# Expert weights in another buffer order, with two 4 MB loads for the second half of the second pair's gate/up rows

## The reference

```python
h = rmsnorm(x, norm2_g) * (1 + sc2) + sh2
logits = h @ w_router + b_router              # 32 experts, top 4 per token, softmax over those
for e in range(32):
    gu = h @ w_gu[e] + b_gu[e]                # w_gu[e]: 1024 x 2048 float32, 8 MB
    g, u = split(gu)                          # clamped
    hdn = (u + 1) * (g * sigmoid(1.702 * g))
    y = hdn @ w_down[e] + b_down[e]           # w_down[e]: 1024 x 1024 float32, 4 MB
    acc = acc + comb[:, e] * y
x = x + g2 * acc
```

## Time and profile before

| | us |
|---|---|
| median of 3 runs | 1290.95 |
| lowest and highest run | 1288.82, 1293.2 |
| the profiled execution | 1290.43 |
| its span, first to last instruction | 1288.7 |
| PE busy | 1212.8 (94%) |
| DVE busy | 407.5 (32%) |
| ACT busy | 200.6 (16%) |
| POOL busy | 33.1 (3%) |
| moved by DMA | 475.21 MB, mean 369 GB/s |

### The profile page before, as it was taken

How to read it: one execution, slowest core, us unless ns; L and a number is a source line. 1 busy time by engine, 2 the same in 40 slices (tenths; PEclk the granted TensorE clock), 3 DMA queues, 4 the chain that set the end, 5 groups by cost and what they waited for, 6 DMA issues and landing times.

```text
span 1288.7 us, 14118 instructions
## 1 busy us (share of the span) xinstructions
PE 1212.8 (94%) x5542; PEld 581.2 (45%) x5542; DVE 407.5 (32%) x781; ACT 200.6 (16%) x402; POOL 33.1 (3%) x50
## 2 busy tenths in 40 slices
PE   5999999999999999999999998989999998989997
PEld 1777478888644343333333333433333333334332
DVE  5178895895312211130121112121301211121213
ACT  3222004230221010011101001100111010011000
POOL 3300100001000000000000000000000000000000
PEclk9999999999999999999999999999999999999999
DMA  9943442779599899999999999999999999999995
GB/s 376 379 176 132 137 169 95 311 289 385 229 379 426 347 428 430 425 429 426 426 430 428 428 426 429 426 429 426 429 426 426 429 429 428 426 428 425 429 425 232
DMA packets 53539, 475.21 MB, mean 369 GB/s; under 512 B 3986, under 2 KB 4146, under 8 KB 23939
## 3 DMA queue, kind: packets, MB, share of 16 engines
q1 hardware_dynamic: 52370, 471.26, 88.1%
q0 software_dynamic: 1136, 3.51, 0.9%
HBM read 473.70 MB, written 1.05 MB: 368 GB/s over the span
## 4 chain that ended last, share of the span: by engine, by line
PE 67%; DMA 28%; DVE 2%; ACT 1%; issue 1%; SPq 0%; DVEq 0%
PE bank L1170 20%; PE bank L1269 12%; DMA area_sb<-w_down 11%; DMA ring_sb<-w_down 11%; PE bank L874 10%; PE bank L1125 4%; PE bank L1285 4%; PE bank L1028 3%; PE bank L883 3%; DMA area_3h_sb<-w_down 3%; DMA ring_sb<-w_gu 2%; PE bank L1069 2%; PE bank L1139 1%; DVE area_sb L1896 1%; PE bank L799 1%
## 5 line engine op out<-in xcount | busy, mean ns | idle before, releaser
L1170 PE MATMUL bank<-ring_sb,area_sb 128*64 128x512 f32 x1152 | 341.5, 599 | 5.6 <-DMA area_3h_sb<-w_gu 5.4
L1170 PE MATMUL bank<-area_sb 128*64 128x512 f32 x768 | 232.5, 599 | 11.4 <-DMA ring_sb<-w_gu 11.4
L1269 PE MATMUL bank<-ring_sb,area_sb 128*64 128x512 f32 x512 | 175.9, 603 | 22.6 <-DMA area_sb<-w_down 7.2
L1170 PEld LDWEIGHTS bank<-ring_sb,area_sb 128*64 128x64 f32 x1152 | 103.6, 137 | 137.9 <-issue 136.1
L874 PE MATMUL bank<-area_3h_sb,ring_sb 128*128 128x256 f32 x704 | 154.2, 379 | 0.0
L874 PEld LDWEIGHTS bank<-area_3h_sb,ring_sb 128*128 128x128 f32 x704 | 133.2, 190 | 20.1 <-issue 1.8
L1170 PEld LDWEIGHTS bank<-area_sb 128*64 128x64 f32 x768 | 70.3, 138 | 158.8 <-issue 158.8
L1269 PE MATMUL bank<-area_sb 128*64 128x512 f32 x352 | 109.1, 600 | 10.5 <-DMA area_sb<-w_down 10.5
L2155 DVE TENSOR_SCALAR area_sb<-bank 128x512 f32<-128x512 f32 x32 | 22.1, 691 | 278.1 <-PE bank L1170 278.1
L1269 PEld LDWEIGHTS bank<-ring_sb,area_sb 128*64 128x64 f32 x512 | 51.8, 138 | 121.7 <-issue 104.3
L2179 DVE TENSOR_TENSOR area_sb<-area_sb,bank 128x512 f32<-128x512 f32 x64 | 44.0, 687 | 172.8 <-PE bank L1285 172.8
(11 more groups left out here) (281 smaller groups left out, 882.7 us busy)
## 6 DMA issues: line engine op xcount, KB each, us to landing
ring_sb<-w_gu SPq DMA_DIRECT2D x72, 2048.0 KB, 30.4
area_sb<-w_gu SPq DMA_DIRECT2D x48, 2048.0 KB, 26.3
ring_sb<-w_down SPq DMA_DIRECT2D x32, 2048.0 KB, 30.4
area_sb<-w_down SPq DMA_DIRECT2D x22, 2048.0 KB, 20.7
ring_sb<-w_in SPq DMA_DIRECT2D x14, 2048.0 KB, 10.5
ring_sb<-w_ada SPq DMA_DIRECT2D x12, 2048.0 KB, 10.6
area_3h_sb<-w_down SPq DMA_DIRECT2D x8, 2048.0 KB, 39.0
area_3h_sb<-w_gu SPq DMA_DIRECT2D x8, 2048.0 KB, 39.1
```

The costliest lines, as they stand in the source:

```text
L1170: ins = pe.matmul(bank[n][r, :], xT[:, k, r], w[e][:, n * 512:(n + 1) * 512], start=False, stop=k == KT - 1, skip_group_check=True)
L1269: ins = pe.matmul(bank[4 + n][r, :], hidT[:, k, e * SLOTS:(e + 1) * SLOTS], w[e][:, kk // 2, kk % 2, n * 512:(n + 1) * 512], start=False, ...
```

## The change

1. `SLOT_OF` is a new order of the buffers, so that chunks 16 and 18 (the second half of the gate/up rows of pair b's first expert) lie in buffers 0 and 1 and chunks 17 and 19 (those of its second expert) in 2 and 3, side by side.
2. In all bodies but the last, each of these two pairs of chunks is one load of 4 MB (`load_four_rows`), issued in the place of chunk 16 and of chunk 17, once both buffers are free; chunks 18 and 19 have no load of their own. PE waits for all four before k 4 of pair b and no more at k 6.
3. Channels are interleaved by four: partition p holds rows 4p to 4p + 3 of 512. The 4 MB load thus has 32 KB in one stretch for each partition; the other gate/up loads take two of the four rows, 16 KB out of each 32 KB. The turns, the gathers, the modulation columns, the router's rows and its gain follow with a step of 4.
4. Eight chunks instead of ten are loaded ahead in the loop (`AHEAD`). Before the first body ten loads are still issued, in the order `FIRST_AHEAD`: chunks 0 to 7, 12 and 13, which go to buffers 0 to 9. The first body is written out, without the loads that have been made.
5. The last turn of h2 waits for the last piece of x before its first transpose, where two of its four could start a piece earlier.

```diff
@@ -49,7 +49,10 @@
 PAIR_CHUNKS = 12
 BODY_CHUNKS = 2 * PAIR_CHUNKS
-SLOT_OF = list(range(MOE_SLOTS)) + list(range(7)) + [7, 8, 9] + [3, 4, 5, 6]
+SLOT_OF = [0, 1, 2, 3, 4, 5, 6, 7] + [0, 1, 2, 3, 8, 9, 4, 5] + [0, 2, 1, 3, 6, 7, 8, 9]
+AHEAD = 8
+FIRST_AHEAD = [0, 1, 2, 3, 4, 5, 6, 7, 12, 13]
 FAR = 4096.0
 F32 = mybir.dt.float32
@@ -518,10 +521,13 @@
         def moe_chunk_landed(b, c):
             return moe_landed[SLOT_OF[PAIR_CHUNKS * b + c]]
-        def wait_moe_chunk(eng, i, b, c):
+        def wait_moe_chunk(eng, i, b, c, p):
             n = PAIR_CHUNKS * b + c
-            eng.wait_ge(moe_chunk_landed(b, c), i * (16 * SLOT_OF.count(SLOT_OF[n]))
-                        + 16 * SLOT_OF[:n + 1].count(SLOT_OF[n]))
+            slot = SLOT_OF[n]
+            fewer = slot in (SLOT_OF[PAIR_CHUNKS + 6], SLOT_OF[PAIR_CHUNKS + 7])
+            eng.wait_ge(moe_landed[slot], i * (16 * (SLOT_OF.count(slot) - fewer)) + fewer * 16 * p
+                        + 16 * SLOT_OF[:n + 1].count(slot))
         def moe_bank(name):
             return bank[6 + MISC_NO[name] % 2]
@@ -610,69 +616,96 @@
                 e0 = j * 4 + 2 * b
                 e = c % 2
+                flat = moe_flat[SLOT_OF[PAIR_CHUNKS * b + c]]
                 if c < 8:
-                    row = 2 * P * (c // 2)
-                    src = a["w_gu"][0, bass.ds(e0 + e, 1), row:row + 2 * P, :]
+                    rows = slice(W * (c // 4), W * (c // 4 + 1))
+                    src = a["w_gu"][0, bass.ds(e0 + e, 1), rows, :].rearrange("e (p k) m -> p e k m", k=4)
+                    src = src[:, :, c // 2 % 2 * 2:c // 2 % 2 * 2 + 2, :]
+                    if flat is None:
+                        flat, src = moe_slot(b, c), src.rearrange("p e k m -> p (e k) m")
+                    else:
+                        src = src.rearrange("p e k m -> p (e k m)")
                 else:
                     row = 4 * P * ((c - 8) // 2)
                     src = a["w_down"][0, bass.ds(e0 + e, 1), row:row + 4 * P, :]
-                flat = moe_flat[SLOT_OF[PAIR_CHUNKS * b + c]]
-                if flat is not None:
-                    sp.dma_start(flat, src.rearrange("e (p k) m -> p (e k m)", p=P))\
-                        .then_inc(moe_chunk_landed(b, c), 16)
-                elif c < 8:
-                    sp.dma_start(moe_slot(b, c), src.rearrange("e (p k) m -> p (e k) m", k=2))\
-                        .then_inc(moe_chunk_landed(b, c), 16)
-                else:
-                    sp.dma_start(moe_slot(b, c), src.rearrange("e (p h k) m -> p (e h) (k m)", h=2, k=2))\
-                        .then_inc(moe_chunk_landed(b, c), 16)
+                    if flat is None:
+                        flat, src = moe_slot(b, c), src.rearrange("e (p h k) m -> p (e h) (k m)", h=2, k=2)
+                    else:
+                        src = src.rearrange("e (p k) m -> p (e k m)", k=4)
+                sp.dma_start(flat, src).then_inc(moe_chunk_landed(b, c), 16)
+            def load_four_rows(i, j, c):
+                n = PAIR_CHUNKS + c
+                first = (NF + SLOT_OF[n]) % WEIGHT_SLOTS
+                src = a["w_gu"][0, bass.ds(j * 4 + 2 + c % 2, 1), W:D, :].rearrange("e (p k) m -> p (e k m)", k=4)
+                sp.dma_start(ring[:, first:first + 2, :].rearrange("p s m -> p (s m)"), src)\
+                    .then_inc(moe_chunk_landed(1, c), 16)
             def load_step(c, j):
-                src = a["w_gu"][0, bass.ds(j * 4 + 2, 2), 6 * P:8 * P, :]\
-                    .rearrange("e (p k) m -> p e k m", k=2)[:, :, c - 6, :]
+                src = a["w_gu"][0, bass.ds(j * 4 + 2, 2), W:D, :]\
+                    .rearrange("e (p k) m -> p e k m", k=4)[:, :, 2 + c - 6, :]
                 sp.dma_start(moe_slot(1, c), src)\
                     .then_inc(moe_chunk_landed(1, c), 16)
             def load(i, j, n, last=False):
-                wait_slot(i, n)
+                if not last and n in (PAIR_CHUNKS + 4, PAIR_CHUNKS + 5):
+                    wait_slot(i, n + 2)
+                elif last or n not in (PAIR_CHUNKS + 6, PAIR_CHUNKS + 7):
+                    wait_slot(i, n)
                 if last and n >= BODY_CHUNKS - 2:
                     load_halves(n % PAIR_CHUNKS, j)
                 elif last and n in (PAIR_CHUNKS + 6, PAIR_CHUNKS + 7):
                     load_step(n % PAIR_CHUNKS, j)
+                elif not last and n in (PAIR_CHUNKS + 4, PAIR_CHUNKS + 5):
+                    load_four_rows(i, j, n % PAIR_CHUNKS)
+                elif not last and n in (PAIR_CHUNKS + 6, PAIR_CHUNKS + 7):
+                    pass
                 else:
                     load_moe(n // PAIR_CHUNKS, n % PAIR_CHUNKS, j)
-            def body(i, j, last):
-                for n in range(MOE_SLOTS, BODY_CHUNKS):
-                    load(i, j, n, last)
+            def body(i, j, last=False, loaded=()):
+                for n in range(AHEAD, BODY_CHUNKS):
+                    if n not in loaded:
+                        load(i, j, n, last)
                 if not last:
-                    for n in range(MOE_SLOTS):
+                    for n in range(AHEAD):
                         load(i + 1, j + 1, n)
-            def one_pass(p, first=False):
-
-                i0 = p * BODIES
-                for n in range(MOE_SLOTS):
-                    if not first:
-                        wait_slot(i0, n)
-                    elif n < 4:
-                        wait_freed(NF + n - WEIGHT_SLOTS)
-                    elif n == 4:
+            def first_loads():
+                for n in FIRST_AHEAD:
+                    slot = SLOT_OF[n]
+                    if slot < 4:
+                        wait_freed(NF + slot - WEIGHT_SLOTS)
+                    elif slot == 4:
                         sp.wait_ge(merge_done, 1)
-                    elif n == 6:
+                    elif slot == 6:
                         sp.wait_ge(products_ready, JOB["mod2T3"] + 1)
-                    elif n in (7, 8):
-                        wait_freed(NF + n - 3 - WEIGHT_SLOTS)
-                    elif n == 9:
+                    elif slot in (7, 8):
+                        wait_freed(NF + slot - 3 - WEIGHT_SLOTS)
+                    elif slot == 9:
                         sp.wait_ge(products_ready, JOB["logits1"] + 1)
                     load_moe(n // PAIR_CHUNKS, n % PAIR_CHUNKS, 0)
-                with sp.Fori(0, BODIES - 1) as j:
-                    body(i0 + j, j, False)
-                body(i0 + (BODIES - 1), BODIES - 1, True)
+            def one_pass(p, first=False):
+                i0 = p * BODIES
+                if first:
+                    first_loads()
+                    body(i0, 0, loaded=FIRST_AHEAD)
+                else:
+                    for n in range(AHEAD):
+                        wait_slot(i0, n)
+                        load_moe(n // PAIR_CHUNKS, n % PAIR_CHUNKS, 0)
+                with sp.Fori(1 if first else 0, BODIES - 1) as j:
+                    body(i0 + j, j)
+                body(i0 + (BODIES - 1), BODIES - 1, last=True)
             one_pass(0, first=True)
             sp.wait_ge(flag_ready, 1)
@@ -745,10 +778,10 @@
             mix_kernel(0)
             mix_kernel(1)
-            pool.dma_start(w_router.rearrange("p (c d) m -> p c d m", d=2),
-                           a["w_router"][0].rearrange("(c p d) m -> p c d m", p=P, d=2)).then_inc(router_landed, 16)
-            pool.dma_start(gain2.rearrange("p (c d) -> p c d", d=2),
-                           a["norm2_g"][0].rearrange("(c p d) -> p c d", p=P, d=2)).then_inc(gain2_landed, 16)
+            pool.dma_start(w_router.rearrange("p (c d) m -> p c d m", d=4),
+                           a["w_router"][0].rearrange("(c p d) m -> p c d m", p=P, d=4)).then_inc(router_landed, 16)
+            pool.dma_start(gain2.rearrange("p (c d) -> p c d", d=4),
+                           a["norm2_g"][0].rearrange("(c p d) -> p c d", p=P, d=4)).then_inc(gain2_landed, 16)
             pool.dma_start(b_router[:, :], a["b_router"].to_broadcast([P, EXPERTS])).then_inc(router_landed, 16)
             pool.wait_ge(products_ready, JOB["hyT21"] + 1)
...
@@ -1072,13 +1104,10 @@
             def turn_h2(t, c):
                 b = job(f"h2T{t}{c}")
+                pe.wait_ge(x1_made, 2 * t + c + 1 + (t and c))
                 for k in range(4):
-                    if t == 0 or c == 0:
-                        pe.wait_ge(x1_made, 2 * t + c + 1)
-                    else:
-                        pe.wait_ge(x1_made, 4 + k // 2)
-                    first = c * W + 2 * P * (k // 2) + k % 2
-                    ins = pe.transpose(b[:, k * P:(k + 1) * P], x[:, t, first:first + 2 * P - 1:2], ident[:, :])
+                    ins = pe.transpose(b[:, k * P:(k + 1) * P], x[:, t, c * W + k:c * W + k + 4 * P - 3:4],
+                                       ident[:, :])
                 end(ins)
             def raw_logits(t):
@@ -1120,9 +1149,9 @@
                 pe.wait_ge(h2_ready, 3 + g)
```

(46 more changed lines are left out.)

## The result

| | before | changed |
|---|---|---|
| median of 4 runs each, us | 1291.47 | 1303.04 |
| lowest and highest | 1288.82, 1293.2 | 1302.9, 1306.94 |
| the profiled execution | 1290.43 | 1306.94 |
| its span | 1288.7 | 1305.0 |
| PE busy | 1212.8 | 1268.2 |

The ratio is 1.0095, with a 95% interval of 1.0078 to 1.0112: slower by 0.95%, where 0.31% less was forecast. The profiled execution is the slowest of the four; between the two medians lie 11.6 us. Its front part already ran 3.3 us late: SP issued the second w_out load at 288.24 us, before at 284.95, and PE's first gather starts at 362.08, before at 358.78. So of the 16.3 us between the two spans some 13 lie behind the front part.

The account below looks back on a forecast made before the run. The prediction took the DMA transfers to bound the expert stage. From 1290.43 us, - 2.8 (second gap) - 1.7 (packets) + 0.5 (tail) = - 4.0 gave 1286.4, with the median 0.5 higher at 1286.9 us; range 1282.5 to 1291.5.

Parts of the forecast that it names:

- Interleave by four: Strided operands of turns and gathers step by 4 instead of 2: cost 0, or 0.7 us at 15 ns more a product.
- Second gap, made smaller: Transfer gap at 415 to 450 us shrinks from 5.7 (6.0 by the windows) to 3.0 us: gain taken as 2.8 us.
- Fewer packets: The 4 MB loads and fewer buffer 6 fillings save 26 packets of 9.4 ns, 0.24 us a body: 1.7 us in all.
- rival 1: 32 KB runs are no cheaper than two of 16 KB: total - 2.8, 1288.1 us; chance 0.15.
- rival 3: Gate/up loads taking 16 KB out of each 32 KB of HBM run slower; at 2.5%, 1298.7 us; chance 0.12.
- Steady order: In the full stream, 4 MB loads don't starve the queue: margin 5 us, cost 0; PE waits once a body, 7.6 us.
- The tail: After the last long wait PE sets the end: 0.3 late, + 1.7 for clock, - 1.5 for a drop gone, together + 0.5.
- first term: In the tail, the clock stays low behind PE's 7.6 us wait, costing + 1.7 us (0 to 3.4).
- the drop at the end: The clock drop behind PE's 1.95 us wait for chunk 21 in the last body goes away: - 1.5 us.
- rival 2: The clock costs twice: more than 3.4 us, say 6.8, at 1.2 GHz behind the long wait; 1288.6 us; chance 0.10.

Follow-up runs that it names:

- e2: The kernel before with only the gathers' step changed from 2 to 4, no load, buffer or wait changed: ratio 1.0096 to the kernel before.
- e7: The changed kernel with a different step in each of a body's four gathers (1, 3, 8 and 4): 1294.73 us in its one run.
- e1: The changed kernel with h2 stored regrouped so that the gathers load contiguous columns: ratio 0.9982 to the kernel before, median 1289.39 us beside 1290.9.
- e3: e1 with its 4 MB loads replaced by 2 MB loads, each behind its own buffer's release: ratio 0.9989 to the kernel before.
- e6: The changed kernel's buffer order and eight ahead, but interleave by two, 2 MB loads in one stretch, gathers at step 2: ratio 0.9987 to the kernel before.
- e5: e1 with its 4 MB loads made of 16 KB runs, same place and waits: ratio 0.9992 to the kernel before.
- e8: e1 with the last body but one written out and its chunks 16 to 19 loaded as 2 MB loads: ratio 0.9968, median 1287.48 us beside 1291.64.

## Why the prediction was wrong

**The step that failed** is "Interleave by four": "Cost 0; if each of the 3 x 16 gather products before the stream is full cost 15 ns more, 0.7 us." It measured 3.7 us for each pair's gather of 16 products, 0.23 us a product where 15 ns was the most that I allowed; that is 7.4 us a body, and some 12 us in the end (e2 alone: 12.3 between the medians). I took the turns as the nearest row: they load their strided operand in 207 ns at step 4 (a mean, the median is 211) and 209 at step 2. That is so after the change too (212 and 214 at step 4), but a turn is another operation than the gather's matmul, and its row did not bound the gather's. Nor is a step free for a turn. The turns of contiguous columns in the kernel before, which the earlier trace rows doesn't have, load in 140 ns:

```profile
L1212 PEld LDWEIGHTS bank<-ident_sb,area_sb x32: 137/140/144, 383.8 to 1252.3; 128*128 128x128 f32 x32
```

So a turn pays some 70 ns at step 2 already and nothing more at step 4, and rows at steps 2 and 4 alone could not show it. The bound from both sides was not one: the gathers' own row (196 ns at step 2, next to 190 for the contiguous loads of the front part) tells nothing of step 4, and I should have let it cost up to twice as much. Then PE's body would have come out at 109.85 + 2 x 4.0 = 117.9 us, equal to the transfers', and the rival on the slower side would have been there. Why a turn and a gather pay so differently was not tried.

The Trainium skill has the rule (SBUF — State Buffer, "Door 1: The DMA port swizzle"): SBUF is read in lines of 16 bytes, and at least two hits on a line are needed for full speed. The gathers' loads agree: 196 ns at step 2 (the kernel before), 329 at 4 and 335 at 8 (e7). The same note goes on that one can stride for free as far as 4 float32; here the measurement decides, and a step of 4 isn't free.

**What held**, by the prediction's own terms, in the versions with the gathers mended:

- *Second gap, made smaller*, with the gathers mended only: e1 moves 411 GB/s in the window 375 to 415 us and 419 in 415 to 450, 2.2 us missing for 6.0 before; 3.0 was forecast.
- *Fewer packets*: right to the hundredth. Before, landings are 117.70 us apart; one filling less of buffer 6 gives 117.6 (e3, e6), 4 MB loads of 16 KB runs 117.61 (e5), 32 KB runs 117.45 (e1). The last step is 0.15 us for 16 packets, 9.4 ns each, so rival 1 falls. The prediction's estimate of 3.5 ns, worked out from the Trainium skill (DMA: Bandwidth & Descriptors, "Why small descriptors are slow (HBM only)" and "Where 436 GB/s comes from"), falls too: by it the step would be 0.06 us.
- *The spaced reads* (rival 3) cost nothing: e3 with them and e6 without them land at the same distance.
- *Steady order*: with the gathers mended the 4 MB loads starve no queue (428 GB/s from 450 to 1250 us in e1). The long wait came in six bodies, from the second on and not from the third, with 5.9 us on average and 8.2 at most; 7.6 was forecast.

**The tail** had the right mechanism for its first term and the wrong size. "With the 0.3 that is + 0.5": PE took 131.1 us for the way that I put at 127.9 + 1.7, since the clock lost 2.6 us behind the long wait, not 1.7, and the last body waits 1.3 us for ACT, not 0.7 as in body 0. And the drop at the end (- 1.5) did not go in e1: PE no longer idles there for a transfer, but the wait for ACT is left, and the clock fell behind it all the same. That wait doesn't decide it alone. With the same 1.3 us in front of them the 16 products take 5.35 us in the changed kernel, e1 and e5, and 3.65 in e2, e7 and e8; what decides was not found. So of the stream's 5 us 2.0 arrived in the span: in e1 the stream has some 0.2 us left in the window from 1267 us (above), before it still had 0.4 in the one from 1272:

```profile
1272.00:1273.00 1.00, 1.00 (x8) 0.29 (x4) 0.00 (x0) 0.00 (x0) 0.00 (x0) 1.00 0.37 152
```

This is close to rival 2, true beside the failed step. In the changed kernel itself it has no part: PE never waits there for a transfer.

Not settled: the front part differs by up to 3.3 us from one trace to the next, before the experts begin. It is late in the traces of the changed kernel, e2, e5 and e8 and not in the others, which goes with no edit; I did not look for its cause.

## What to carry to other kernels

A change of layout that pays in the transfers is paid for by every engine that reads the layout: list each read with its operand's role, and price it from a row of the same operation and role, or leave it up to twice as long. An engine with 7% to spare is not free to take 7% more: its lead over the bound is what absorbs the start, so two resources that are equally long per turn cost the lead once. Loads that land together make one long wait of several short ones; where the last of them stands shortly before the end, the work that the clock loses behind it (2.6 us in e1) is in the open. Loading the last turn in small pieces again is worth a try: it gave the lowest ratio here, though not clear of e1's.

## What the runs showed of the hardware

- The load of a 128 x 128 float32 stationary operand takes 192 ns contiguous, 196 at step 2, 261 at step 3, 329 at step 4 and 335 at step 8; a transpose's load takes 140 ns contiguous and some 210 at steps 2 and 4.
- The transfers' cost of 9.4 ns for a packet and DMA engine, taken from 2 and 16 KB runs, holds at 32 KB (e5 and e1: 0.15 us for 16 packets).
- Reads of 16 KB out of every 32 KB of HBM are as fast as contiguous ones (117.61 us a body for both, e6 and e3).
- Behind an idle 6.6 us of PE the granted clock stayed at 0.50 for 5.2 us of work; behind 1.95 us, for about 3. Behind 1.3 us it fell in three traces and stayed at 1.00 in three others.
- DVE reading float32 at a step of 4 takes 0.68 us for 128 x 512, contiguous 0.49.
